# Another order for the first octet of S5 and for the attention steps of a two-layer decoder trunk

## What is computed

```
h = x
h = h + S5(rmsnorm(h));         h = h + mlp(rmsnorm(h))      # layer 0
K, V = rmsnorm(h) @ W_kv + b_kv                              # 4 heads of 64
h = h + attention(rmsnorm(h), K, V); h = h + mlp(rmsnorm(h)) # layer 1
out = rmsnorm(h)
```

## Time and profile before

| | us |
|---|---|
| median of 3 runs | 1064.45 (1062.7 to 1065.29) |
| the profiled execution, its own time | 1064.73 |
| its span, first to last instruction | 1062.7 |
| PE busy | 1031.7, 97% of the span |
| DVE, ACT, POOL busy | 571.3, 227.8, 694.7 |

### The profile page before, as it was taken

The page is one execution under the profiler, slowest core; times in us unless marked ns, Lnnn a source line. Parts: engine busy times, 40 slices in busy tenths (PEclk is TensorE's granted clock), DMA queues, the critical chain, the costliest instruction groups (busy, mean ns, idle before and its releaser), DMA issues.

```text
span 1062.7 us, 15744 instructions
## 1 busy us (share of the span) xinstructions
PE 1031.7 (97%) x5736; PEld 842.5 (79%) x5736; DVE 571.3 (54%) x661; ACT 227.8 (21%) x512; POOL 694.7 (65%) x568
## 2 busy tenths in 40 slices
PE   8699999999999999999999998999999999999996
PEld 3577888888888888888887776888888888888886
DVE  6895354677316514713856886477761372274125
ACT  6773211111001000101312777221100010010011
POOL 6996876587667766766646330588776676676650
PEclk9799999999999999999999998999999999999999
DMA  6123332233333222223223110133323222222212
GB/s 245 27 45 114 112 112 97 67 113 99 100 99 99 99 97 87 95 99 100 99 80 99 41 42 18 60 103 115 99 99 98 89 91 98 99 99 99 99 60 80
DMA packets 35906, 97.52 MB, mean 92 GB/s; under 512 B 11145, under 2 KB 13705, under 8 KB 35601
## 3 DMA queue, kind: packets, MB, share of 16 engines
q1 hardware_dynamic: 35856, 96.83, 27.7%
HBM read 92.36 MB, written 2.10 MB: 89 GB/s over the span
## 4 chain that ended last, share of the span: by engine, by line
PE 87%; DVE 7%; issue 3%; ACT 2%; POOL 0%; DVEq 0%; ACTq 0%; POOLq 0%
PE ps L1252 24%; PE ps L1254 23%; PE ps L1253 23%; PE ps L1208 2%; PE ps L1209 2%; PE ps L1210 2%; PE ps L1395 1%; PE ps L1383 1%; PE ps L1409 1%; PE ps L1076 1%; PE ps L1315 1%; PE ps L1314 1%; PE ps L1313 1%; PE ps L1098 1%; ACT s_sb L645 1%
## 5 line engine op out<-in xcount | busy, mean ns | idle before, releaser
L438 POOL TENSOR_TENSOR w_lo<-raw,w_hi 128x1024 fp32r<-128x1024 f32 x164 | 415.0, 2530 | 13.7
L1252 PE MATMUL ps<-hid,w_hi 128*128 128x512 f32 x704 | 275.8, 392 | 0.0
L1253 PE MATMUL ps<-hid,w_hi 128*128 128x512 f32 x704 | 274.0, 389 | 0.0
L1254 PE MATMUL ps<-hid,w_lo 128*128 128x512 f32 x704 | 274.0, 389 | 0.0
L350 POOL TENSOR_TENSOR gate_sb<-gate_sb 128x1 f32<-128x1 f32 x164 | 40.8, 249 | 315.2 <-PE ps L1254 275.8
L1252 PE MATMUL ps<-act,w_hi 128*128 128x512 f32 x464 | 180.6, 389 | 0.0
L1254 PE MATMUL ps<-act,w_lo 128*128 128x512 f32 x464 | 180.5, 389 | 0.0
L1253 PE MATMUL ps<-act,w_hi 128*128 128x512 f32 x464 | 180.5, 389 | 0.0
L435 POOL TENSOR_SCALAR w_hi<-raw 128x1024 fp32r<-128x1024 f32 x164 | 173.2, 1056 | 0.0
L1252 PEld LDWEIGHTS ps<-hid,w_hi 128*128 128x128 f32 x704 | 132.1, 188 | 30.6 <-issue 3.2
L1254 PEld LDWEIGHTS ps<-hid,w_lo 128*128 128x128 f32 x704 | 132.1, 188 | 27.8
(11 more groups left out here) (215 smaller groups left out, 1078.9 us busy)
## 6 DMA issues: line engine op xcount, KB each, us to landing
raw<-panels_in SPq DMA_DIRECT2D x164, 512.0 KB, 3.3
xy<-xu_in SPq DMA_DIRECT2D x4, 512.0 KB, 7.5
out<-h SPq DMA_DIRECT2D x8, 256.0 KB, 2.2
prm<-prm_in SPq DMA_DIRECT2D x1, 1280.0 KB, 5.9
h<-x_rows_in SPq DMA_DIRECT2D x1, 1280.0 KB, 13.0
h<-x_rows_in SPq DMA_DIRECT2D x1, 768.0 KB, 7.4
dd<-dd_in SPq DMA_DIRECT2D x1, 256.0 KB, 5.8
toep<-k_even SPq DMA_DIRECT2D x4, 64.0 KB, 2.3
```

The costliest lines, as they stand in the source:

```text
L438: nc.gpsimd.tensor_tensor(w_lo[:, s, :], raw[:, s % 2, :], w_hi[:, s, :].bitcast(F32), ALU.subtract).then_inc(w_split, 1)
L1252: mm(ps[:, bank, :], w_hi[:, s, w], x[:, 0, k, :], start=(k == 0), stop=False)
L1253: mm(ps[:, bank, :], w_hi[:, s, w], x[:, 1, k, :], start=False, stop=False)
L1254: last = mm(ps[:, bank, :], w_lo[:, s, w], x[:, 0, k, :], start=False, stop=(k == KT - 1))
```

## The change

S5's first octet:
- ACT: `decay` (L543) is written before `turn_t`; the copies of `lag0_weights(0)` to `(2)` stand after the squares of octets 1, 3 and 5 instead of before all squares; the root (L546) stands before `evacuate_v(0)`; `copy_p(1)` and `evacuate_v(1)` stand before `evacuate_k(0)`.
- POOL: `project_im(1)` stands before the rest of octet 0's weights, and the product `dd` after `inputs(0)` instead of before it.
- DVE: all four frames stand before `run_states(0)`.
- PE: 5 matmuls on zeros instead of 7 before the transposes of `turn8`, and one more after them; `lags(0)` stands after `turns(3)` and `sums(0)`.

Attention: PE's step is scores(Q), mix(Q-3), turn_p(Q-2), dense(Q); the buffers of scores and of their maxima and sums are three (`DEEP`) instead of two; ACT's and DVE's stages of a step are in another order, and `next_queries` has a lag of 1. W_o's units 0 to 3 run up to k-tile 6 in steps 11 to 18, instead of up to 4 or 6 in steps 11, 12, 16, 17 and after the last.

```diff
-WARM = 7
+WARM = (5, 1)
...
-        s_sb = sb("s_sb", [P, 2, 4, 2 * BLK + 1], where=over)
+        s_sb = sb("s_sb", [P, DEEP, 4, 2 * BLK + 1], where=over)
...
             project_im(0)
+            project_im(1)
             weights_mul(0, (1, 2))
             weights_sum(0)
+            wait(pool, setup_a, SETUP_RSTD)
+            inputs(0)
             wait(pool, s_dd, 16)
             tt(dd[:, 0], dd[:, 0], dd[:, 1], mul).then_inc(setup_p, 1)
-            wait(pool, setup_a, SETUP_RSTD)
-            inputs(0)
-            project_im(1)
             weights_mul(1)
...
+            a.wait_ge(setup_a, SETUP_R8)
+            act_fn(decay[:, :, 1:], r8[:].unsqueeze(2).to_broadcast([P, GP, NK - 1]), ACT.Copy).then_inc(decayed, 1)
             wait(a, turn_mm, 1)
             act_fn(turn_t[:], ps[0:8, 3, :], ACT.Copy).then_inc(turn_copied, 1)
             wait(a, s_prm, 16)
-            for o in range(SETUP_LAG0):
-                lag0_weights(o)
...
+                if o % 2 == 1 and o // 2 < SETUP_LAG0:
+                    lag0_weights(o // 2)
...
             copy_p(0)
-            a.wait_ge(setup_a, SETUP_R8)
-            act_fn(decay[:, :, 1:], r8[:].unsqueeze(2).to_broadcast([P, GP, NK - 1]), ACT.Copy).then_inc(decayed, 1)
-            evacuate_v(0)
             wait(a, setup_v, SETUP_MS)
             act_fn(rstd_u[:, 0], rstd_u[:, 1], ACT.Sqrt).then_inc(setup_a, 1)
+            evacuate_v(0)
             frame(0)
+            copy_p(1)
+            evacuate_v(1)
             evacuate_k(0)
             frame(1)
             for o in range(NO):
-                if o + 1 < NO:
+                if 0 < o < NO - 1:
                     copy_p(o + 1)
...
-            skewed([(turned, 2), (o_hi, 3), (norm_p, 1), (exps, 0)])
+            skewed([(norm_p, 1), (o_hi, 3), (turned, 2), (exps, 0)])
...
-            frame(1)
+            for c in range(1, 4):
+                frame(c)
             run_states(0)
-            frame(2)
-            frame(3)
...
-            skewed([(turned, 2), (denominators, 1), (maxima, 0), (o_low, 3), (next_queries, 0)])
+            skewed([(denominators, 1), (maxima, 0), (next_queries, 1), (turned, 2), (o_low, 3)])
...
-            for _ in range(WARM):
+            for _ in range(WARM[0]):
                 mm(ps[:, 3, :], idle[:, 0:P], idle, start=True, stop=True)
...
+            wait(pe, setup_v, SETUP_INV)
+            for _ in range(WARM[1]):
+                mm(ps[:, 6, :], idle[:, 0:P], idle, start=True, stop=True)
             turns(0)
...
             turns(1)
-            lags(0)
             turns(2)
             fold(1)
+            turns(3)
             sums(0)
-            turns(3)
+            lags(0)
...
-            early, middle = range(0, 4), range(4, 6)
...
-            beside[last_quad - 4] = [(out_unit, 0, early)]
-            beside[last_quad - 3] = [(out_unit, 1, early)]
-            beside[last_quad + 1] = [(out_unit, 2, early), (out_unit, 0, middle)]
-            beside[last_quad + 2] = [(out_unit, 3, early), (out_unit, 1, middle)]
+            for step, work in ((-4, [(0, 0, 2)]), (-3, [(0, 2, 4)]), (-2, [(1, 0, 2)]), (-1, [(1, 2, 4)]), (0, [(0, 4, 6)]),
+                               (1, [(1, 4, 6), (2, 0, 2)]), (2, [(2, 2, 6)]), (3, [(3, 0, 6)])):
+                beside[last_quad + step] = [(out_unit, m, range(k, end)) for m, k, end in work]
...
-            skewed([(scores, 0), (dense, None), (mix, 2), (turn_p, 1)])
-
-            out_unit(2, middle)
-            out_unit(3, middle)
+            skewed([(scores, 0), (mix, 3), (turn_p, 2), (dense, None)])
```

More of the change, by code:

```diff
@@ L33 @@
 HD = 64
+DEEP = 3
 NQ = 16
@@ L200, in build @@
         v_sb = sb("v_sb", [P, NBLK, NKV * HD], where=over)
-        s_sb = sb("s_sb", [P, 2, 4, 2 * BLK + 1], where=over)
+        s_sb = sb("s_sb", [P, DEEP, 4, 2 * BLK + 1], where=over)
         mask = sb("mask", [P, 2 * BLK], where=over)
[L204 to L207, removed]
+        mx = sb("mx", [P, DEEP, 4], where=over)
+        negm = sb("negm", [P, DEEP, 4], where=over)
+        den = sb("den", [P, DEEP, 4], where=over)
+        rden = sb("rden", [P, DEEP, 4], where=over)
         over.close()
@@ L640, in exps @@
             def exps(Q):
-                u, n, q = Q // NBLK, Q % NBLK, Q % 2
+                u, n, r = Q // NBLK, Q % NBLK, Q % DEEP
                 a.wait_ge(m_step, 3 * Q + 3)
@@ L644, in exps @@
                 for j in range(4):
-                    act_fn(s_sb[:, q, j, at], s_sb[:, q, j, at], ACT.Exp, bias=negm[:, q, j:j + 1],
-                           accum_out=den[:, q, j:j + 1]).then_inc(p_exp, 1)
+                    act_fn(s_sb[:, r, j, at], s_sb[:, r, j, at], ACT.Exp, bias=negm[:, r, j:j + 1],
+                           accum_out=den[:, r, j:j + 1]).then_inc(p_exp, 1)
             def norm_p(Q):
-                u, n, q = Q // NBLK, Q % NBLK, Q % 2
+                u, n, r = Q // NBLK, Q % NBLK, Q % DEEP
                 a.wait_ge(rden_done, Q + 1)
                 for j in range(4):
-                    act_fn(s_sb[:, q, j, window(n)], s_sb[:, q, j, window(n)], ACT.Copy,
-                           scale=rden[:, q, j:j + 1]).then_inc(p_norm, 1)
+                    act_fn(s_sb[:, r, j, window(n)], s_sb[:, r, j, window(n)], ACT.Copy,
+                           scale=rden[:, r, j:j + 1]).then_inc(p_norm, 1)
             def turned(Q):
@@ L1015, in maxima @@
             def maxima(Q):
-                u, n, q = Q // NBLK, Q % NBLK, Q % 2
+                u, n, r = Q // NBLK, Q % NBLK, Q % DEEP
                 sink = COLS("sink")[:, 4 * u:4 * u + 4]
-                ts(s_sb[:, q, :, 2 * BLK:], sink.unsqueeze(2), 1.0, None, ALU.mult).then_inc(m_step, 1)
+                ts(s_sb[:, r, :, 2 * BLK:], sink.unsqueeze(2), 1.0, None, ALU.mult).then_inc(m_step, 1)
                 v.wait_ge(s_mm, Q + 1)
-                tt(s_sb[:, q, :, window(n)],
+                tt(s_sb[:, r, :, window(n)],
                    ps[:, 0:2, :].rearrange("p e (t m) -> p (e t) m", t=2)[:, :, window(n)],
@@ L1025, in maxima @@
                 v.wait_ge(m_step, 3 * Q + 1)
-                nc.vector.tensor_reduce(mx[:, q], s_sb[:, q, :, window(n).start:], AX.X, ALU.max).then_inc(m_step, 1)
+                nc.vector.tensor_reduce(mx[:, r], s_sb[:, r, :, window(n).start:], AX.X, ALU.max).then_inc(m_step, 1)
                 v.wait_ge(m_step, 3 * Q + 2)
-                ts(negm[:, q], mx[:, q], -1.0, None, ALU.mult).then_inc(m_step, 1)
+                ts(negm[:, r], mx[:, r], -1.0, None, ALU.mult).then_inc(m_step, 1)
             def denominators(Q):
-                u, n, q = Q // NBLK, Q % NBLK, Q % 2
+                u, n, r = Q // NBLK, Q % NBLK, Q % DEEP
                 v.wait_ge(p_exp, 4 * Q + 4)
-                nc.vector.reciprocal(rden[:, q], den[:, q]).then_inc(rden_done, 1)
+                nc.vector.reciprocal(rden[:, r], den[:, r]).then_inc(rden_done, 1)
             def turned(Q):
@@ L1092, in turns @@
                    ).then_inc(frame_mm, 1)
+            wait(pe, setup_v, SETUP_INV)
+            for _ in range(WARM[1]):
+                mm(ps[:, 6, :], idle[:, 0:P], idle, start=True, stop=True)
             turns(0)
-            wait(pe, setup_v, SETUP_INV)
             for o in range(NO):
@@ L1394, in turn_p @@
                         at = (j % 2) * 2 * BLK + b * BLK
-                        last = turn(ps[:, 4 + j // 2, at:at + BLK], s_sb[:, q, j, b * BLK:(b + 1) * BLK], ident)
+                        last = turn(ps[:, 4 + j // 2, at:at + BLK], s_sb[:, r, j, b * BLK:(b + 1) * BLK], ident)
                 last.then_inc(pt_mm, 1)
```

## The result

The changed kernel takes 1058.61 us (median of 6 runs, 1057.04 to 1059.65); the kernel before, beside it, 1063.63 (6 runs): ratio 0.9949, 95% interval 0.9937 to 0.9960. It is 5.0 us faster. The forecast was 1059.9 in 1056.8 to 1063.5.

A forecast was written before the change was run, and what follows sets the result against it. PE was taken as the bound, busy 97% of the span, so gains come only from its holes and half-clock time: 1064.73 - 2.4 (S5) - 2.2 (attention) = 1060.1, about 1059.9 on the median's scale; range 1056.8 to 1063.5.

The forecast's parts named there:

- Said 2.2 (1.4 to 3.1): Attention's term: 2.2 us gained; 3.1 as worked out, 1.4 if the hole at scores(4) brings half clock.
- PE's work does not change: scores 1.06, transposes 1.02: Attention: PE's scores, transposes, mix and tiles keep their times, so only holes and half clock, 8.1 us, could be had.
- New wait 2.3 us: Attention, scores(4): PE waits 2.3 us for the later next_queries, 1.2 if the sink copy doesn't meet POOL's `w_lo`.
- If the hole at scores(4) makes the clock fall: Attention: 3.4 us at half level after that hole would cost 1.7, leaving 1.4 us of the 3.1 gain.
- No tile comes before its `ot_lo`: Attention, W_o tiles in steps 11 to 18: quad 0 is done at step 10 and used at 11.
- said 2.4: S5's term: 2.4 us gained, between 3.3 and 1.2 if the squares meet half clock; outer bounds 0 and 4.5.
- Rival B: One half falls away: S5 gains 0.5 or attention's holes bring half clock, gain 0; 1061.2 to 1064 us, chance 0.27.
- Before they took 9.18 us, because the clock was at its half level: S5's head: the eight squares, dense now, end at 17.7; mean square 4.2 us earlier, 2.4 with half clock.
- the 52.13 of the states: S5, DVE: `run_states(2)` was at 52.13 us in the profile before and was forecast at 48.0.
- The reciprocal was said for 19.3: S5's head: the mean square done at 19.3 us, or 21.0 with half clock, instead of 23.47.
- 1.1 us each, 2 at half clock: S5, PE: `fold(1)` at 23.3, `turns(3)` and `sums(0)` take 1.1 us each, 2 at the half clock expected there.
- Each then repeats octets of 8.0 and 7.9 us, to the end: S5: DVE keeps about 4 us of lead and POOL 2.4, carried through equal octets to the end.

The follow-up runs named there:

- PE kept at work (5): The changed kernel with four matmuls of 384 columns on constants, results unused, in PE's holes before turns(2) and fold(1): 1054.93 us, ratio 0.9923 against the kernel before.
- Experiment 9: The changed kernel with PE's attention step as scores, dense, mix, turn_p, so dense matmuls no longer follow transposes: 1063.14 us, ratio 0.9994 against the kernel before.
- experiment 10: The changed kernel with W_o's first tiles back at the old steps: 1063.35 us, ratio 0.9990 against the kernel before.
- experiment 1: The new S5 alone, with attention's order, lags, buffers and W_o tiles as in the kernel before: 1064.52 us, ratio 0.9997 against that kernel.
- experiment 12: The changed kernel plus four extra constant matmuls, with DVE's next_queries between denominators and maxima: 1065.85 us, ratio 1.0009 against the kernel before.

## Why the prediction came out right

| trace | GLU starts | from there to the last group |
|---|---|---|
| before | 90.95 | 962.86 |
| new S5 alone | 92.37 | 962.77 |
| the change | 88.49 | 957.99 |
| new attention alone | 88.38 | 958.00 |
| new attention, old S5, filled warm-up | 91.68 | 958.00 |
| the change, `evacuate_k(0)` first | 90.71 | 958.05 |
| the change, PE kept at work (5) | 85.78 | 958.10 |

**Attention: right in sign, half the size.** Said 2.2 (1.4 to 3.1), measured 4.9: every trace with the new attention has 958.0 us behind the start of the GLU, both with the old 962.8. By its steps:
- "PE's work does not change: scores 1.06, transposes 1.02": this is the mis-sized term, which was set at nothing. 14 more blocks of transposes have dense matmuls behind them, 0.17 each, 2.4 us. Experiment 9 takes 13 of them back.
- "New wait 2.3 us" at scores(4): 1.30. The wait is there and for what was named, but the copy of the sinks of block 3 took 0.21 us and met only the very end of `w_lo`, and the prediction itself gave 1.2 for that case. At scores(12) 1.05 (1.3 said), at mix(13) 1.78 (1.9 said); the wait of 0.77 ahead of mix(0) was not seen. Sum 4.9 instead of 5.5.
- "If the hole at scores(4) makes the clock fall": it was 1.00 throughout attention, also behind the hole of 1.78, where 2.3 us had been followed by half clock in before's trace. In experiment 10 it fell again.
- "No tile comes before its `ot_lo`", the spreading of the tiles: worth 4.5 us by experiment 10, the largest single part.

Of the 4.9, 2.4 are the transposes and 0.4 the holes; I put the other 2.1 down to the half clock that is gone, which the prediction had at up to 2.7. The prices of experiments 9 and 10 (3.8 and 4.5) don't add up to 4.9: each brings holes back, and 10 the half clock with them, so they overlap.

**S5: said 2.4, measured 0.0 to 0.6.** The ratio of S5 alone allows a gain of at most 1.5 us (0.9986). Rival B had named the mechanism ("the Toeplitz DMAs set S5's pace"), at 0.5 us. The step that failed is the base of the sum: "Before they took 9.18 us, because the clock was at its half level", and the 52.13 of the states. Both are from one execution. Where the same code had full clock, those states started at 49.5, and there the new order is 0.2 us ahead. Three more of its steps were off:
- The reciprocal was said for 19.3 and came at 20.53, with reduction and squares on time: L793 took 1.11 us instead of 0.20, up to the end of the first of POOL's two sums, which start at 18.64. With the old order of POOL the two sums lie at 17.7 to 20.2, so this step would have met them there too: what is new is that it comes early enough. The Trainium skill, "GPSIMD Engine Reference", Specifications, has the rule: POOL shares its SBUF interfaces with VectorE and contends with those VectorE instructions that use a two-port mode or two SBUF inputs. The rows agree, and show it for the TENSOR_SCALAR alone: the TENSOR_REDUCE ahead of it took its 0.69 and the RECIPROCAL behind it, beside the second sum, its 0.55.
- Half clock lasted from 23 to 33 us, longer than the "1.1 us each, 2 at half clock"; `k_even` came 1.4 us later than said (35.6 against 34.2), `outputs(0)` 1.0 (42.16 against 41.2), and the states of octet 2 at 49.30 against 48.0.
- "Each then repeats octets of 8.0 and 7.9 us, to the end" held for DVE: in all but one of the fourteen traces the states of octet 2 to 6 start 8.0 us apart. It left out what PE waits for. In the six traces in which the last transfers of octets 3 to 6 land on time (see below), the GLU starts 38.8 to 39.4 us behind the states of octet 2. In the changed kernel's own trace, where two are late by 1.4 and 0.7 us, it is 39.2; in the other seven it is 40.4 to 42.1.

So the two errors, 2.7 us too little and about 2 too much, cancelled. The number was right by luck; its halves were not right.

**The late transfers.** The spread of executions, some 2 to 4 us, lies in the first 92 us: behind them traces with the same attention agree within 0.15. In seven of the fourteen the last `k_even` transfer of octet 4 lands 3.2 to 3.9 us after its issue instead of 1.8. One of the seven is the changed kernel's own (3.2); the other six start the GLU 0.8 to 4.1 us later than the trace of the nearest kernel without it. The traces name a companion. The DMA list has a second queue, with single transfers of 16 KB that it calls "instruction"; here are the two queues (packets, MB, share of the DMA engines) in experiment 1, from the issue of that transfer at 69.70 to its landing at 73.43:

```profile
q1 hardware_dynamic: 464, 0.12, 18.7%
q8 instruction: 1, 0.02, 2.0%
```

The same stretch in before's trace, 70.52 to 72.34, has no q8 line. Over all fourteen traces I took the last Toeplitz transfer of octets 1 to 7, 98 of them: 24 landed after more than 2.2 us, and in all 24 a q8 transfer had started between 0.5 us ahead of their issue and 1.9 behind it. Of the 74 that landed within 2.0 us, none had one between 0.5 ahead and 1.7 behind. So a transfer is late, by this reading, when an instruction transfer happens to fall into its time.

**What stays open.** That the q8 transfer holds up the other is read from their coincidence; no run moves it by itself. Why S5 alone gains nothing in 12 runs, when its trace has full clock in the squares, is explained by late transfers in one trace (3.7 us in octet 4, 3.2 in octet 6); that they make up the median is only argued. An estimate from the table supports it: from the GLU's start to a run's time there are 962.8 + 10.9 us with the old attention, so the twelve runs (1061.85 to 1065.96) had it at 88.2 to 92.3, four of them up to 89.1 and eight from 90.3 on.

## What to carry to other kernels

Take one profiled execution for a mechanism, not for a baseline: if a stage's length hangs on the clock, ask what the old code does at full clock before you credit the new one. Before you move work forward, fill PE's idle stretch ahead of the chain: four matmuls without use gave 2.8 us by the ratios (3.7 by the medians), more than the whole reordering of S5. And before you move a stage on DVE, list who waits for the stage behind it, PSUM banks included: to save two visible waits, 2.4 us together, cost 9 to 11.

## What the runs showed of the hardware

- 128x128 fp32 transposes, eight in a block, hold PE 0.85 us if dense matmuls follow and 1.02 if scores or mix do; four hold it 0.41 and 0.59. The number of columns isn't what decides: `turns(1)` has 512 columns and starts 0.97 us behind the eight transposes of `fold(0)` (17.91 to 18.88 in the changed kernel), as late as `lags` with 128 columns behind those of a later `fold` (52.28 to 53.24). Transposes and dense matmuls both use tiles of `128*128`; scores (`64*128`), mix and `lags` (`128*64`) and `turns` (`8*128`) do not. That the change of tile is the price fits all these rows; no run isolates it.
- DVE's TENSOR_SCALAR from SBUF to SBUF waits for POOL's running instruction to end: 1.11 us instead of 0.20 and 2.25 instead of 0.14 beside a TENSOR_TENSOR, 2.60 instead of 0.49 too (the queries' L1009 at 598.87 in experiment 12), and 1.03 instead of 0.17 beside `w_hi`'s TENSOR_SCALAR (581.75 in the changed kernel).
- ACT loaded the table for the root at 18.17 in 1.28 us, before the instruction's wait was over (root at 20.57): a switch ahead of a wait was free.
- A small DMA (8 KB) that shared its time with a 16 KB transfer of the instruction queue landed after 2.3 to 3.9 us instead of 1.8, 24 times of 24.
